# Stepping the on-chip buffers of an encoder-block kernel by 32 to 128 bytes

## What is computed

```python
h = _rmsnorm(x, norm_g[layer])
proj = h @ w_in[layer]                          # 512 x 2048 by 2048 x 10304
aq, ak, av, ag, cq, ckv, kr, bg, mg = jnp.split(proj, SPLIT_POINTS, axis=-1)
...
oa = _diff_attention(aq[..., 0, :], aq[..., 1, :], ak[..., 0, :], ak[..., 1, :], av, pos_f, lam, slopes)
oa = _rmsnorm(oa, a_subln_g[layer], SUBLN_EPS) * (1.0 - lam_init)
ya = (oa.reshape(b, s, A_WIDTH) * jax.nn.silu(ag)) @ w_oa[layer]
q = (_rmsnorm(cq, q_norm_g[layer]) @ w_uq[layer]).reshape(b, s, B_HEADS, B_NOPE + B_ROPE)
kv = (_rmsnorm(ckv, kv_norm_g[layer]) @ w_ukv[layer]).reshape(b, s, B_HEADS, B_NOPE + B_V_DIM)
...
ob = _mla_attention(q_nope, q_rope, k_nope, k_rope, vb)
yb = (ob.reshape(b, s, B_WIDTH) * jax.nn.silu(bg)) @ w_ob[layer]
ga, gb = jnp.split(mg, 2, axis=-1)
merged = jax.nn.sigmoid(ga) * ya + jax.nn.sigmoid(gb) * yb
x = x + merged @ w_out[layer]
return _rmsnorm(x, final_g)
```

## Time and profile before

| | us |
|---|---|
| median of three runs | 1430.2 |
| the profiled execution, its own time | 1429.3 |
| its span from first to last instruction | 1427.5 |
| PE busy | 1413.2 (99%) |
| PEld busy | 1175.1 (82%) |
| DVE busy | 1020.0 (71%) |
| ACT busy | 707.1 (50%) |
| POOL busy | 31.5 (2%) |
| mean granted clock of TensorE, share of full speed | 0.999 |
| bytes moved by DMA | 218.43 MB, mean 153 GB/s |

### The profile page before, as it was taken

One profiled execution on the slowest core, in us unless ns is written; L12 is line 12 of the kernel. 1 busy time (PEld: TensorE's weight loads), 2 busy tenths in 40 slices (PEclk: granted clock), 3 DMA queues, 4 the chain that ended last, 5 costly groups with the idle time before them and its releaser, 6 DMA issues.

```text
span 1427.5 us, 17881 instructions
## 1 busy us (share of the span) xinstructions
PE 1413.2 (99%) x6604; PEld 1175.1 (82%) x6604; DVE 1020.0 (71%) x1381; ACT 707.1 (50%) x894; POOL 31.5 (2%) x52
## 2 busy tenths in 40 slices
PE   8999999999999999999999999999999999999997
PEld 7888888888888888888888878888888888888886
DVE  6967898798878868677667656666676353478966
ACT  6546334544344456665666667555564222324434
POOL 0000000000000000000000000000000000000000
PEclk9999999999999999999999999999999999999999
DMA  8439576766756543222222434322242444617674
GB/s 300 145 125 316 177 263 186 236 213 212 238 184 207 184 146 83 79 82 81 81 81 82 114 106 133 84 72 66 81 140 74 151 125 152 207 45 247 197 254 172
DMA packets 182976, 218.43 MB, mean 153 GB/s; under 512 B 19456, under 2 KB 133248, under 8 KB 182272
## 3 DMA queue, kind: packets, MB, share of 16 engines
q1 hardware_dynamic: 174304, 197.64, 44.5%
q10 hardware_dynamic: 8608, 19.93, 3.6%
HBM read 195.51 MB, written 22.02 MB: 152 GB/s over the span
## 4 chain that ended last, share of the span: by engine, by line
PE 91%; DVE 3%; DMA 1%; ACT 1%; issue 1%; SPq 1%; POOL 0%; DVEq 0%; POOLq 0%; ACTq 0%
PE duo L2115 28%; PE duo L2117 28%; PE duo L2116 28%; PE duo L2168 2%; DMA start_y<-start_columns 1%; PE duo L2142 1%; PE duo L2145 1%; SPq L610 1%; ACT m_hi L886 1%; PE duo L2159 1%; PE duo L2164 1%; PE duo L2163 1%; PE duo L2160 1%; PE duo L2161 1%; PE duo L2598 0%
## 5 line engine op out<-in xcount | busy, mean ns | idle before, releaser
L1385 DVE TENSOR_TENSOR w_lo<-w_raw,w_hi 128x1024 fp32r<-128x1024 f32 (+1 forms) x116 | 135.3, 1167 | 99.3 <-ACT w_hi L781 98.7
L2115 PE MATMUL duo<-h_hi,w_hi 128*128 128x512 f32 x512 | 201.8, 394 | 0.0
L2117 PE MATMUL duo<-h_hi,w_lo 128*128 128x512 f32 x512 | 199.6, 390 | 0.0
L2116 PE MATMUL duo<-h_lo,w_hi 128*128 128x512 f32 x512 | 199.6, 390 | 0.0
L886 ACT ACTIVATE m_hi<-m_raw 128x2048 fp32r<-128x2048 f32 (+1 forms) x66 | 115.5, 1752 | 144.6 <-PE duo L2117 71.5
L781 ACT ACTIVATE w_hi<-w_raw 128x1024 fp32r<-128x1024 f32 (+1 forms) x118 | 119.2, 1011 | 124.3 <-DMA w_raw<-in_w_ob_dram 65.8
L1502 DVE TENSOR_TENSOR m_lo<-m_raw,m_hi 128x2048 fp32r<-128x2048 f32 (+3 forms) x71 | 141.9, 2001 | 26.9 <-ACT m_hi L886 26.5
L2115 PE MATMUL duo<-m_hi,h_hi 128*128 128x512 f32 x368 | 144.6, 393 | 1.6 <-DVE h_lo L1538 0.9
L2117 PE MATMUL duo<-m_hi,h_lo 128*128 128x512 f32 x368 | 143.3, 389 | 0.0
L2115 PE MATMUL duo<-m_hi,s_hi 128*128 128x512 f32 x320 | 124.5, 389 | 0.0
L2117 PE MATMUL duo<-m_hi,s_lo 128*128 128x512 f32 x320 | 124.5, 389 | 0.0
(11 more groups left out here) (322 smaller groups left out, 2991.0 us busy)
## 6 DMA issues: line engine op xcount, KB each, us to landing
m_raw<-in_w_in_dram SPq DMA_DIRECT2D x110, 512.0 KB, 4.7
w_raw<-in_w_in_dram SPq DMA_DIRECT2D x132, 256.0 KB, 3.0
o_raw<-in_w_out_dram SPq DMA_DIRECT2D x32, 512.0 KB, 5.1
spare<-in_w_in_dram SPq DMA_DIRECT2D x17, 512.0 KB, 4.6
h_raw<-in_w_in_dram SPq DMA_DIRECT2D x17, 512.0 KB, 4.9
w_raw<-in_w_oa_dram SPq DMA_DIRECT2D x32, 256.0 KB, 3.3
sig<-gates SPq DMA_DIRECT2D x8, 1024.0 KB, 6.3
w_raw<-in_w_ob_dram SPq DMA_DIRECT2D x32, 256.0 KB, 3.4
```

Of the source, the lines that this page charges most:

```text
L1385: dve.tensor_tensor(w_lo[:, piece.slot, 0:cols], w_raw[:, piece.slot, 0:cols], w_hi[:, piece.slot, 0:cols].bitcast(F32), ALU.subtract).the ...
L2115: pe.matmul(dst, lhs_hi, rhs_hi, start=start, stop=False)
L2116: pe.matmul(dst, lhs_hi, rhs_lo, start=False, stop=False)
L2117: return pe.matmul(dst, lhs_lo, rhs_hi, start=False, stop=stop)
```

## The change

A table `STAGGER` gives places in kilobytes and steps in bytes. `at` adds to a buffer's address all steps whose place is at or below the buffer's own. To make room for the 1,024 bytes that the steps add up to, `base` is rounded up to 512 bytes instead of 2 KB and falls to 16,896 bytes.

```diff
+STAGGER = ((32, 64), (64, 64), (96, 64), (112, 64), (128, 64), (144, 64), (160, 64), (164, 32), (168, 96), (182, 64),
+           (198, 128), (200, 32), (202, 96), (204, 128))
...
-        base = (nc.sbuf_base + 2 * KB - 1) // (2 * KB) * (2 * KB)
+        base = (nc.sbuf_base + 511) // 512 * 512
...
         def at(name, kb, shape, dt=F32):
-            return nc.alloc_sbuf_tensor_at(name, shape, dt, offset=base + int(kb * KB))
+            stagger = sum(step for place, step in STAGGER if kb >= place)
+            return nc.alloc_sbuf_tensor_at(name, shape, dt, offset=base + int(kb * KB) + stagger)
...
-        assert base + 206 * KB - 336 <= nc.sbuf_usable_end
+        assert base + 206 * KB - 336 + sum(step for _, step in STAGGER) <= nc.sbuf_usable_end
```

## The result

| | before | after |
|---|---|---|
| median, us | 1430.2 (1429.12 to 1430.27, four runs) | 1455.99 (1454.9 to 1456.89, four runs) |
| ratio | | 1.0182, 95% interval 1.0169 to 1.0195 |
| span of the profiled execution | 1427.5 | 1454.6 |

The prediction was 1430.2 us with a range of 1,422 to 1,440. The kernel is 25.8 us slower, and the range doesn't hold it.

A forecast was written before the change was run, and what follows sets the result against it. The prediction took PE to bound the kernel, busy 1413.2 of 1427.5 us. Its terms, 0 on PE, 0 on the other engines and 0 on DMA, left the median at 1430.2 us, with a range of 1,422 to 1,440.

The forecast's parts named there:

- PE as the bound, and the count: Whole kernel: PE busy 1413.2 of 1427.5 us; about 5,750 matmuls of 512 columns, one nanosecond each is 5.75 us.
- The third rival: 512-column matmuls: distance 0 is free of collisions, others may not be; at worst 9 ns each, 52 us, 1,482; 9%.
- What is removed: Distance 0 between stationary and moving operand: taken as 0 us saved, 5.75 us at most.
- a lone matmul of 388 ns: PE's wait for DVE at 146.5 us: no load beside it, against 389 with one, so a load costs 1 ns at most.
- the first rival: All matmuls: the 13.3 ns excess is a collision and goes, 76 us plus about 4 on shorter ones, 1,350 us; 9%.
- The 12.3 ns: Every 512-column matmul: about 12.3 of the 13.3 ns over 213.3 are there without any load, so no distance removes them.
- The circle argument: Loads beside matmuls: the two reads pass through every distance modulo 512 whatever the start, so a shift of 64 bytes changes nothing.
- The uneven matmuls: First matmuls behind a break, 230 to 240 ns apart: under 3 us in all, which the change could remove or double; taken as 0.
- DVE and ACT: Other engines on the same memory: no collisions now, same durations after within 1%, `w_lo` at 1224 ns; 0 us.
- Transfers: DMA to buffers off multiples of 512 bytes: taken as 0 us, with `start_y` landing in about 15 us.
- The rival: First weights and `start_y`: transfers to odd addresses take a quarter more, 3.7 us, 1,434; twice that for half more; 8%.
- The comparison inside the profile: `m_lo` with `s34_lo` keeps distance 0, with `s12_lo` gets 64: same starts forecast, 226 to 227 ns apart.

The follow-up runs named there:

- m1_distances: Kernel of its own without the encoder: TensorE rows of 32 matmuls, stationary operand moved against moving one; fp32r 226.65 ns at 0 bytes, 233.4 at 64.
- m4_entries: Kernel without the encoder: rows of 20 fp32r matmuls at 0, 64, 160 or 192 bytes, entered from other distances; at 0 all settle at 226.67 ns.
- all64: Changed kernel with one step only, 64 bytes under everything, so all distances modulo 512 stay 0: 1429.64 us, ratio 0.9998 to the kernel before.
- w64: Changed kernel with two steps only, buffers between 96 and 128 KB 64 bytes off all others modulo 256: 1448.32 us, ratio 1.0129.
- w192: Changed kernel with two steps only, buffers between 96 and 128 KB 192 bytes off all others modulo 256: 1446.26 us, ratio 1.0107.

## Why the prediction was wrong

- **PE as the bound, and the count** held: 5,671 matmuls by 5.0 ns are 28.4 us, and the span grew by 27.1. The third rival, which had 9%, is what happened in its effect: distance 0 was the cheap one, and the others cost 5.0 ns a matmul instead of its worst case of 9. That two reads take turns, as it supposed, no run shows.
- **What is removed** is the step that failed: it put the change of the distance at 0, and the runs showed 5.0 ns on each of 5,671 matmuls. It read a lone matmul of 388 ns as proof that the distance can't matter. One part came out: the first rival's 76 us weren't to be had by addresses, since no set of 512 was under 226.67 ns. But the lone matmul doesn't show that either. It says nothing of other distances, all operands of the kernel before being at multiples of 512 bytes. "Different operands at many distances, and one price" was one distance seen many times. And the length of a lone matmul isn't a price without the load: it is 388 to 397 ns in m1_distances, and 397 at 16.40 us in the trace that the prediction was read from. The 12.3 ns that "are there without any load" rest on it and have no other support.
- **The circle argument** failed with it. It had the load's read pass every distance to the moving read, so that only the mean could count. But 4 bytes already cost 5.7 ns, and at distance 0 a load of a quarter of the columns costs no less. The price hangs on the exact offset and on what stood before in the row, not on how long the reads run beside each other. It even assumed a load that reads evenly, which no run shows.
- **The uneven matmuls** The earlier trace rows were the hint that was put aside. Their size before came out: the mean of 227.19 ns against the settled 226.66 makes 3.0 us, and the prediction had "under 3 us". What it missed is that they could become the rule. Rows at distance 0 that m4_entries enters from other distances start with the same 224 to 236 ns before they settle, so I take them for the same state; the changed kernel doesn't settle at 226.7.
- **DVE and ACT** were right: line L1390, which was L1385, has the same median, and ACT is busy for 707.3 us after 707.1.

```profile
L1390 DVE TENSOR_TENSOR w_lo<-w_raw,w_hi x116: 680/1224/1228, 494.7 to 1261.3; 128x1024 fp32r<-128x1024 f32 x104, 128x512 fp32r<-128x512 f32 x12
```

- **Transfers** were right in size: `start_y` took 15.74 us after 15.24, and DVE's last wait is still for PE, 2.04 us after 1.51, so that transfer doesn't set the end. (`start_y` takes 15.67 us in all64 and 14.0 in w64 and w192, so its time doesn't follow its own place alone.) all64 shows no loss of time with every address moved. The rival had a quarter more on a transfer; the 6% on `w_raw` is what the landing times show, and it stays hidden. (Its "twice that" for a half more, 7.4 us, doesn't fit the 8.9 us that the prediction works out for the same case further down.)

```profile
1447.01 0.69 DVE L2096 TENSOR_TENSOR last_x<-duo,last_x 128x512 f32<-128x512 f32 x1 [2.04 <-PE duo L2122]
```

- **The comparison inside the profile** was announced with the wrong reading, that by new collisions the pair at distance 0 would stay cheap. With `s34_lo`, whose load has distance 0 to `m_lo`, those matmuls of `m_lo` have a mean of 234.1 ns, and with `s12_lo`, at 64, of 229.4 (226.8 and 226.5 before). The pair at distance 0 is the dearer one: it stands between others that are not.

## What to carry over

Before anyone moves buffers against each other, a row of the two operands alone at a few distances gives the price: here 0 modulo 256 bytes was the best of all distances tried for 512-column matmuls of fp32r with full stationary tiles. Two quite different tables of fourteen steps cost 1.8 and 1.7%, and shifting one group of buffers cost 1.3 and 1.1%. A trace in which all addresses are alike can't tell what the alignment is worth, however many pairs it has. A single instruction's length is no measure of a row; take the distance of starts over some thirty of them. And a forecast that is summed from steady prices misses what neighbours do to each other, even where its total comes out.

## What the chip showed that I had not expected

- fp32r matmuls of 512 columns stand 226.65 ns apart at distance 0 modulo 256 bytes and 228.9 to 234.3 at others, bf16 ones 215.8 at any. The Trainium skill (SBUF — State Buffer, "Who interferes with whom") gives PE two independent read ports, one for the moving operand and one for weight loads, and says that "PE and ACT never wait on anyone." Loads and moving reads of fp32r were not independent here: moving the stationary one up by 64 bytes costs 6.8 ns a matmul. Which part of the chip makes them wait, no run here shows, nor whether it is the load beside a matmul or its own that counts.
- The row has a memory. In m4_entries distance 0 with full tiles draws it to 226.67 ns from 24 of 24 starts; distance 192 has two steady rhythms, 228.89 and 233.33 ns, and keeps the one it came in with.
- The kernel before pays a little of this already: in the heads the 22 matmuls behind four transposes have a mean of 228.8 ns, not 226.7, since they need some ten matmuls to settle.
- The excess over the 213.3 ns of 512 columns at one a cycle of the full clock, 2.4 GHz, doesn't shrink with the load at distance 0 (32 columns, a load of 109 ns: 231.7 ns a matmul). That it is 20 ns at 448 columns and 13.3 at 256, 320, 384 and 512 stays unexplained.
